# A gated multilayer stage: the down panel's rounding copy is moved ahead of the first half's activation on ScalarE

## The reference

```python
D_MODEL, SEQ, D_FF = 1024, 512, 2816

def modulate(h, shift, scale):
    return h * (1 + scale[:, None, :]) + shift[:, None, :]

def swiglu(h, w_gu, w_down):
    g, u = jnp.split(h @ w_gu, 2, axis=-1)
    return (jax.nn.silu(g) * u) @ w_down

def sandwich(x, fn, g_pre, g_post, shift, scale, gate, res_w):
    h = modulate(rmsnorm(x, g_pre), shift, scale)
    y = rmsnorm(fn(h), g_post)
    return x + res_w * gate[:, None, :] * y

mod = (c_act @ w_ada[l] + b_ada[l]).reshape(b, N_SUB, 3, D_MODEL)
ffn1 = lambda h: swiglu(h, ffn1_w_gu[l], ffn1_w_down[l])
x = sandwich(x, ffn1, norm_pre[l, 0], norm_post[l, 0], mod[:, 0, 0], mod[:, 0, 1], mod[:, 0, 2], 0.5)
x = sandwich(x, mix, norm_pre[l, 1], norm_post[l, 1], mod[:, 1, 0], mod[:, 1, 1], mod[:, 1, 2], 1.0)
x = sandwich(x, ffn2, norm_pre[l, 2], norm_post[l, 2], mod[:, 2, 0], mod[:, 2, 1], mod[:, 2, 2], 0.5)
```

## Time and profile before

| what | us |
|---|---|
| median of three runs | 4395.76 (4394.27 to 4400.28) |
| profiled execution | 4396.47 |
| its span, first to last instruction | 4394.6 |
| busy: PE, DVE, ACT, POOL | 3955.3, 2291.2, 1368.4, 1333.8 |
| mean granted TensorE clock | 0.951 of full |

### The profile page before, as it was taken

How to read it: one execution, slowest core, us unless ns; L and a number is a source line. 1 busy time by engine, 2 the same in 40 slices (tenths; PEclk the granted TensorE clock), 3 DMA queues, 4 the chain that set the end, 5 groups by cost and what they waited for, 6 DMA issues and landing times.

```text
span 4394.6 us, 50811 instructions
## 1 busy us (share of the span) xinstructions
PE 3955.3 (90%) x18628; PEld 3174.8 (72%) x18628; DVE 2291.2 (52%) x3495; ACT 1368.4 (31%) x1832; POOL 1333.8 (30%) x1012
## 2 busy tenths in 40 slices
PE   7999898989997979799879979999797889798999
PEld 6888676867776748558668768888674747577887
DVE  4676744146664361641682267777545352824334
ACT  3222643241214242252112341111424242224223
POOL 2444332433442103003232313322120303434443
PEclk8999999999998999899989989999998999899999
DMA  4454221223331102001111123332110202222222
GB/s 178 172 191 162 77 81 58 93 99 132 143 143 54 39 0 72 20 1 58 58 53 63 58 80 124 122 115 102 44 51 20 72 0 69 76 86 78 95 95 86
DMA packets 57220, 364.68 MB, mean 83 GB/s; under 512 B 5744, under 2 KB 12144, under 8 KB 13936
## 3 DMA queue, kind: packets, MB, share of 16 engines
q1 hardware_dynamic: 42064, 271.11, 17.7%
q10 hardware_dynamic: 15008, 91.49, 5.5%
HBM read 360.49 MB, written 2.10 MB: 83 GB/s over the span
## 4 chain that ended last, share of the span: by engine, by line
issue 68%; POOL 24%; PE 8%; POOLq 0%; DVE 0%; ACT 0%; DVEq 0%; ACTq 0%
POOL b_wlo L561 24%; PE ps L1647 3%; PE ps L1648 3%; PE ps L1649 3%; POOLq L575 0%; DVE b_y L1156 0%; POOLq L577 0%; DVE b_x L1160 0%; DVE b_y L1209 0%; PE ps L1732 0%; ACT b_whi L602 0%; PE ps L1719 0%; ACT b_xout L667 0%; DVE b_stat L1158 0%; POOLq L561 0%
## 5 line engine op out<-in xcount | busy, mean ns | idle before, releaser
L561 POOL TENSOR_TENSOR b_wlo<-b_raw,b_whi 128x512 fp32r<-128x512 f32 x1008 | 1333.6, 1355 | 3040.3 <-ACT b_whi L602 3040.3
L1647 PE MATMUL ps<-b_hhi,b_whi 128*128 128x512 f32 (+1 forms) x3000 | 1110.7, 370 | 42.1 <-DVE b_vp L1548 28.8
L1648 PE MATMUL ps<-b_hlo,b_whi 128*128 128x512 f32 (+1 forms) x3000 | 1101.1, 367 | 0.0
L1649 PE MATMUL ps<-b_hhi,b_wlo 128*128 128x512 f32 (+1 forms) x3000 | 1100.0, 367 | 0.0
L602 ACT ACTIVATE b_whi<-b_raw 128x2048 fp32r<-128x2048 f32 x252 | 480.9, 1908 | 752.1 <-PE ps L1649 735.5
L1647 PEld LDWEIGHTS ps<-b_hhi,b_whi 128*128 128x128 f32 x3000 | 569.6, 190 | 140.3 <-issue 38.6
L1648 PEld LDWEIGHTS ps<-b_hlo,b_whi 128*128 128x128 f32 x3000 | 569.5, 190 | 93.1 <-issue 2.0
L1649 PEld LDWEIGHTS ps<-b_hhi,b_wlo 128*128 128x128 f32 x3000 | 568.8, 190 | 93.5
L1104 DVE SCALAR_TENSOR_TENSOR b_macc<-b_mraw,b_csil,b_macc 128x256 f32<-128x256 f32 x868 | 506.1, 639 | 7.0
L1209 DVE TENSOR_TENSOR b_y<-ps,b_y 128x512 f32<-128x512 f32 x496 | 335.6, 689 | 274.0 <-PE ps L1649 274.0
L1647 PE MATMUL ps<-b_whi,b_dhi 128*128 128x512 f32 x992 | 400.2, 403 | 53.9 <-POOL b_wlo L561 28.1
(11 more groups left out here) (289 smaller groups left out, 5005.7 us busy)
## 6 DMA issues: line engine op xcount, KB each, us to landing
b_raw<-panels SPq DMA_DIRECT2D x252, 1024.0 KB, 4.7
b_mraw<-mod_panels ACTq DMA_DIRECT2D x78, 1024.0 KB, 6.6
b_y<-mod_panels ACTq DMA_DIRECT2D x3, 1024.0 KB, 15.8
b_xin<-xT SPq DMA_DIRECT2D x1, 2048.0 KB, 25.4
b_mraw<-mod_panels SPq DMA_DIRECT2D x2, 1024.0 KB, 19.0
b_rope<-rope ACTq DMA_DIRECT2D x4, 512.0 KB, 3.3
outT<-b_xout SPq DMA_DIRECT2D x4, 512.0 KB, 3.6
b_mod<-mod_panels ACTq DMA_DIRECT2D x1, 1024.0 KB, 20.9
```

What stands on the lines that cost most here:

```text
L561: ins = pool.tensor_tensor(wlo[:, s, c], raw[:, s, c], whi[:, s, c].bitcast(F32), ALU.subtract)
L1647: pe.matmul(out, a[0], b[0], start=first, stop=False)
L1648: pe.matmul(out, a[0], b[1], start=False, stop=False)
L1649: return pe.matmul(out, a[1], b[0], start=False, stop=last)
```

## The change

In gated stages ACT splits the down panel p + 2 right behind the wait for PE's use of panel p, in front of the first half's `hid_lo` wait and silu. Before, it did so in the second half's turn, behind the first half's silu, its wait for DVE's product and its rounding copy. The split of p + 1 stays where it is. The non-gated stages execute the same instructions in the same order.

```diff
@@ -677,10 +677,12 @@
                 for n in range(2):
                     for v in (range(2, mods[1]) if n else range(min(2, mods[1]))):
                         mod_load(mods[0] + v, i, 2 * m.half)
-                    if m.gated or n == 0:
-                        split(p + n + 1, i, m.per_trip)
+                    if n == 0:
+                        split(p + 1, i, m.per_trip)
                     if m.gated or n == 1:
                         act.wait_ge(panel_used, lin(p + (n if m.gated else 0) + 1, m.per_trip, i))
+                        if n == 0:
+                            split(p + 2, i, m.per_trip)
                     else:
                         act.wait_ge(*at("up_first", ("start", st), lin(c + 1, 2, i)))
                     if c >= 1:
```

## The result

| what | before | after |
|---|---|---|
| median, us | 4395.02 (4393.16 to 4400.28, 4 runs) | 4357.52 (4354.79 to 4363.18, 4 runs) |
| ratio | | 0.9914, 95% interval 0.9897 to 0.9932 |
| profiled execution | 4396.47 | 4363.18 |
| its span | 4394.6 | 4361.0 |
| mean granted clock | 0.951 | 0.953 |

The change saves 37.5 us in the medians; 4361 was predicted, 3.5 above the median. "Second unit" begins inside the stage's first unit (at 69.10 and 940.37 us before, 69.44 and 931.81 after) and runs up to the modulation sums (L1670 before, L1672 after) behind its down product; "loop" is what follows up to the last such sums.

A forecast was written before the change was run, and what follows sets the result against it. PE, busy 90% of the span, was taken to lose time only where it stands still or runs at the lower clock. 17.9 + 8.0 + 3.1 + 6.2 + 0 = 35.2 us off 4396.47 gave 4361, range 4352 to 4368.

The forecast's parts named there:

- What bounds the kernel: PE, busy 90%, loses time only standing still or at lower clock; in ffn2 it stands 24.9 us for POOL.
- ffn1's loop: ffn1's eight loop units: third load 1.90 us later, product 1.82 shorter; 0 us, bounds -4 to +15.
- Nine loop units: ffn2's loop: stalls of 1.99 us go, 17.9 us, and five clock drops of 1.59, 8.0 us.
- Who pays for the overlap: POOL's pass over ffn2's second modulation product: DVE loses 4.15 us, the pass takes some 5.6 us.
- ffn1's second unit: ffn1: stall of 3.38 us and clock loss of 2.83 go; gain 6.2 us, bounds 2 to 6.2.
- the rule that I weighed: Two-SBUF-input DVE contends with SBUF-reading GpSimd, second issuer waits entirely; ffn2's DVE then loses 5.58 us for 4.15.
- ffn2's second unit: ffn2: POOL stall of 8.53 us goes, PE stands 4.4 us on DVE's add; 3.1 us net, bounds 0 to 10.4.
- (a): Rival: DVE becomes ffn2's limit, 1 us of ring wait in nine units, clock drops kept; about 4378, chance 0.12.
- (c): Rival: slower, PE waits on late DVE adds for PSUM banks in all 17 loop units; about 4410, chance 0.04.
- (b): Rival: the later third load costs ffn1's loop in full, 15.2 us, another 7 with drops; about 4383, chance 0.07.
- (d): Rival: the panel copy can't start sooner because the raw panel isn't in yet; about 4396, chance 0.03.
- The sum: All terms over ffn1 and ffn2: 35.2 us off the profiled execution's 4396.47, forecast 4361, chance 0.74.

The follow-up runs named there:

- e6: Kernel before, with the second condition vector's accumulations in ffn2 cut to 16 of 256 columns; 4363.01 us, ratio 0.993.
- e9: Changed kernel with four 128x512 ACT copies ahead of the copy of panel p + 1 in ffn2's loop; 4422.09 us in its one run.
- e1: Changed kernel with the panel copy moved in ffn2 alone, ffn1 keeping the old order; 4364.68 us, ratio 0.9933.
- e11: The changed kernel taken again without any edit; 4356.81 us, ratio 0.9917.
- e7: Changed kernel, with the second condition vector's accumulations in ffn2 cut to 16 of 256 columns; 4355.69 us, ratio 0.9909.
- e2: Changed kernel with the panel copy moved in ffn1 alone, ffn2 keeping the old order; 4384.85 us, ratio 0.9979.
- e3: Changed kernel with the moved copy placed behind the first half's silu instead of in front of it; 4356.9 us, ratio 0.9912.
- e4: Changed kernel with eight one-column ACT copies in front of the moved copy in ffn2's loop; 4355.76 us, ratio 0.991.

## Why the prediction was right, and where it was not

- **What bounds the kernel**: right. PE's stalls on POOL in both stages, and the lower clock behind them, were nearly all that the gain came from (0.8 us is ffn1's loop); e6 reached the same 310.90 us from the other end of the chain, by making DVE early instead of ACT's order.
- **Nine loop units**, 25.9 forecast, 27.2 measured. The stall of 1.99 us went in all nine, and the clock drops went with it, as assumed. The unit came to 34.54 for "about 34.7"; nine times this 0.1 to 0.2 is the difference. Part of it is the product itself: 1025.01 - 1014.02 = 10.99 us, where the forecast took the 11.10 of a product that began behind a stall.
- **Who pays for the overlap**: wrong in ffn2, right in ffn1's second unit (DVE's 7.35 us). In ffn2 I took the overlap of the earlier trace rows as "the same pair of operations" and let DVE lose 4.15 us and the pass take 5.6. It was the same pair at another moment of the stream: DVE lost nothing in its products and POOL's pass 2.6 to 2.7 us (7.58 to 7.71 for 5.0). That the sum held all the same is luck: there happened to be room on POOL's side as well, less than I had counted on: the pass ends at 1005.48 + 7.58 = 1013.06 and PE starts at 1014.02 in that unit, 0.96 us later. I had written "done at 1058.2" against 1061.20 and thus counted on 3 us.
- **The Trainium skill**, in the rule that I weighed (SBUF — State Buffer, Who interferes with whom), lets the second to issue wait out the other instruction entirely. In the passes that are held the runs agree: one side loses in full. They go beyond it: POOL's instruction isn't held for one DVE instruction of about 0.47 us but for the rest of the stream, up to 10 us of it; and a pass that began 1.3 us into the stream wasn't held at all, but alternated with it, as did one 6.4 us in that followed another by 0.7 us (e9), and ffn1's.
- **ffn2's second unit**, 3.1 forecast, 2.0 measured in the pair of profiled executions (57.15 us in e1 and 58.82 in e11, which run the same code there, so 1.8 to 3.5; the granted clock over this unit was 0.97 in e1 and 0.94 in the kernel after). The size is near and the mechanism wrong, so this, too, is luck. The step that failed is "the stall on POOL (8.53) goes ... PE starts at 979.5, wants the bank at 983.6 and stands 4.4 us". PE never came to wait for DVE's add there. It waited 5.27 us for POOL again, whose pass took 13.73 us; e7, in which this pass takes 5.26, gives back 7.1.
- **ffn1's second unit**, 6.2 forecast, 6.4 measured: right, stall and lower clock both gone (e2 alone has the same 50.51).
- **ffn1's loop**, 0 forecast, 0.8 saved: right. The third product starts 1.7 us later (20.76 for 19.02 us behind the sums, in the last unit), takes 3.61 us again, as an uncovered one does, and the ring waits went from 4.1 to 3.5 us. A row of DVE in the kernel after:

```profile
415.12 3.61 DVE L1106 SCALAR_TENSOR_TENSOR b_macc<-b_mraw,b_csil,b_macc 128x256 f32<-128x256 f32 x7
```

- **The rivals.** (a) and (c), DVE or the ring becoming the limit, did not come: the nine units have no wait of PE left. DVE could not be the one that pays there; POOL could, and e9 shows what that costs, a kernel slower than before. That rival was missing from my list. (b), the later load, was offset in ffn1 as reckoned. (d) is excluded by the copy at 1037.97.
- **The sum**: 35.2 forecast; the profiled execution came 33.3 lower and the medians 37.5. The profiled one is the slowest of its four, with 3.8 us lost to the clock in mix2's attention.

## What to carry to other kernels

When a copy waits behind a long chain on its engine though its own inputs are ready, look at what it delays if it goes first, and put it behind the first short instruction that starts another engine (e3) rather than in front of it. Where two engines slow each other when they overlap, an overlap seen at one moment is no price for an overlap at another: look for rows in which the one begins in the same place of the other's run of instructions, and where there are none, price both sides, the one held as well as the one that is slowed. A stall of 2 us can cost 3.6 when PE comes out of it at half the clock, so a stall that is removed is worth more than its length.

## What the runs showed of the hardware

- A POOL instruction on two SBUF inputs that came in the midst of an unbroken stream of DVE instructions on two SBUF inputs (128 x 256, one every 0.40 us), when DVE had run undisturbed for 3.02 us or more, waited to the stream's end in every case: up to 10.0 us for one quarter of a pass that otherwise takes 1.29 (e9). DVE didn't lose anything by it (5.62 us for 14 accumulations). Where DVE had run undisturbed for 1.44 us or less, the two took turns: pass 5.58 for 5.0, DVE 9.78 for 5.63; this was so even 6.4 us into a stream, right behind another pass (e9: pass 5.80, DVE 12.85). What decides between the two is left open. The phase inside an instruction does not (e4), and neither a stream with accumulations of 16 columns in it (e7) nor ffn1's, with one accumulation every 0.52 us, held a pass that came 3.0 to 3.5 us behind the last one.
- DVE instructions of 128 x 512 that read one operand from PSUM were not slowed beside a pass (L1194: 0.67 to 0.69 us with it and without); ones with both in SBUF were (L1200: mostly 1.1 to 1.7 us for 0.69).
- Eight copies of one column on ACT, back to back, took 0.76 us in all.
